# Feed-forwards by seven half-size block products for eight, in a two-block transformer kernel

## The reference

```python
hn = rms_norm(h, ln_mlp[layer])
h = h + jnp.square(jax.nn.relu(hn @ w_mlp1[layer])) @ w_mlp2[layer]
...
mod = c_act @ ada_w[layer] + ada_b[layer]
...
h = rms_norm_2(x, norm_mlp[layer]) * (1.0 + scale2) + shift2
x = x + gate2 * (jnp.square(jax.nn.relu(h @ mlp_w1[layer])) @ mlp_w2[layer])
```

## Time and profile before

| what | value |
|---|---|
| runs of the kernel | 2666.81, 2666.29, 2665.3 us; median 2666.29 |
| profiled execution | span 2664.3 us, 35686 instructions; some 2.0 us less than the median of the runs |
| TensorE matmul busy | 2627.4 us (99%), 12468 instructions |
| GpSimd busy | 1944.8 us (73%) |
| VectorE busy | 1268.0 us (48%) |
| ScalarE busy | 806.2 us (30%) |
| the four feed-forwards | from about 326 to 679, 1005 to 1358, 1676 to 2028 and 2309 to 2660 us of the span |

### The profile page before, as it was taken

How to read it: one execution, slowest core, us unless ns; L and a number is a source line. 1 busy time by engine, 2 the same in 40 slices (tenths; PEclk the granted TensorE clock), 3 DMA queues, 4 the chain that set the end, 5 groups by cost and what they waited for, 6 DMA issues and landing times.

```text
span 2664.3 us, 35686 instructions
## 1 busy us (share of the span) xinstructions
PE 2627.4 (99%) x12468; PEld 2069.3 (78%) x12468; DVE 1268.0 (48%) x1836; ACT 806.2 (30%) x1396; POOL 1944.8 (73%) x2832
## 2 busy tenths in 40 slices
PE   9999999999999999999999999999999999999999
PEld 6777788888766678888877888888887666788887
DVE  4766454442476655445234477511223776612211
ACT  4454311002255542101122254300113776401101
POOL 5533599998665559999876866887886555688875
PEclk9999999999999999999999999999999999999999
DMA  5211275653222126566322322333333211233332
GB/s 147 64 48 40 81 223 177 184 175 102 79 63 61 58 87 194 178 191 188 103 88 71 91 63 60 88 103 95 100 90 87 64 56 56 64 111 95 95 95 71
DMA packets 425151, 272.08 MB, mean 102 GB/s; under 512 B 9786, under 2 KB 411588, under 8 KB 425028
## 3 DMA queue, kind: packets, MB, share of 16 engines
q1 hardware_dynamic: 409154, 216.68, 28.1%
q10 hardware_dynamic: 15874, 53.67, 6.4%
HBM read 268.22 MB, written 2.10 MB: 101 GB/s over the span
## 4 chain that ended last, share of the span: by engine, by line
POOL 41%; PE 37%; issue 19%; DVE 1%; POOLq 1%; SPq 1%; DMA 0%; ACT 0%; DVEq 0%; ACTq 0%
POOL w_lo L400 28%; POOL w_hi L393 11%; PE ps L453 5%; PE ps L455 4%; PE ps L454 4%; PE pair L453 4%; PE pair L455 4%; PE pair L454 4%; POOL slot_mark L406 2%; PE ps L2041 2%; PE ps L2043 2%; PE ps L2042 2%; PE ps L1037 1%; PE pair L2451 1%; PE ps L1038 1%
## 5 line engine op out<-in xcount | busy, mean ns | idle before, releaser
L400 POOL TENSOR_TENSOR w_lo<-w_raw,w_hi 128x256 fp32r<-128x256 f32 x1612 | 1329.6, 856 | 33.6
L406 POOL TENSOR_TENSOR slot_mark<-slot_mark 128x1 f32<-128x1 f32 x400 | 98.9, 247 | 653.4 <-PE ps L455 346.8
L393 POOL TENSOR_SCALAR w_hi<-w_raw 128x512 fp32r<-128x512 f32 x806 | 533.6, 681 | 0.0
L453 PE MATMUL ps<-x_hi,w_hi 128*128 128x512 f32 x1040 | 423.5, 407 | 5.1 <-DVE x_lo L944 2.5
L455 PE MATMUL ps<-x_hi,w_lo 128*128 128x512 f32 x1040 | 406.1, 390 | 0.0
L454 PE MATMUL ps<-x_lo,w_hi 128*128 128x512 f32 x1040 | 405.3, 390 | 0.0
L1148 ACT ACTIVATE tt<-sq 128x512 f32<-128x512 f32 x128 | 81.1, 634 | 1029.5 <-DVE sq L1189 525.3
L453 PEld LDWEIGHTS ps<-x_hi,w_hi 128*128 128x128 f32 x1040 | 195.3, 188 | 52.6 <-issue 12.6
L454 PEld LDWEIGHTS ps<-x_lo,w_hi 128*128 128x128 f32 x1040 | 195.5, 188 | 42.5 <-issue 5.5
L455 PEld LDWEIGHTS ps<-x_hi,w_lo 128*128 128x128 f32 x1040 | 195.2, 188 | 42.0
L453 PE MATMUL pair<-x_hi,w_hi 128*128 128x512 f32 x544 | 212.2, 390 | 0.0
(11 more groups left out here) (442 smaller groups left out, 4396.0 us busy)
## 6 DMA issues: line engine op xcount, KB each, us to landing
w_raw<-in_w_mlp_dram SPq DMA_DIRECT2D x128, 512.0 KB, 4.1
w_raw<-in_mlp_w_dram SPq DMA_DIRECT2D x128, 512.0 KB, 4.0
arena<-in_ada_w_dram ACTq DMA_DIRECT2D x96, 512.0 KB, 4.0
w_raw<-in_w_in_ab_dram SPq DMA_DIRECT2D x28, 512.0 KB, 3.7
w_raw<-in_w_qkv_o_dram SPq DMA_DIRECT2D x24, 512.0 KB, 3.7
w_raw<-in_w_qkv_dram SPq DMA_DIRECT2D x24, 512.0 KB, 3.8
w_raw<-in_w_in_e_dram SPq DMA_DIRECT2D x23, 512.0 KB, 4.0
w_raw<-in_w_ple_gate_dram SPq DMA_DIRECT2D x16, 512.0 KB, 4.0
```

What stands on the lines that cost most here:

```text
L393: last = nc.gpsimd.tensor_scalar(w_hi[:, j, k, :], w_raw[:, j, k, :], 1.0, 1.0, ALU.mult, ALU.mult)
L400: last = nc.gpsimd.tensor_tensor(w_lo[:, j, k, :], w_raw[:, j, k, :], w_hi[:, j, k, :].bitcast(F32), ALU.subtract)
L406: nc.gpsimd.tensor_tensor(slot_mark[:, 0:1], slot_mark[:, 1:2], slot_mark[:, 1:2], ALU.subtract)
L453: nc.tensor.matmul(bank[:, :], w_hi[:, j, k, :], hi[:, k, :], start=(k == 0), stop=False)
```

## The change

The first product of a feed-forward is computed in part by a scheme of seven block products for eight (the variant of Strassen's with 15 sums). Of the 32 chunks of the inner width the first six ("std") stay as they were. The other 26 make 13 pairs (hp = 1 to 13). Over a pair the first product is a 2 by 2 block product: the two chunks by the even and the odd tiles of x, by the two halves of the tokens. P1 to P7 are seven products of a 512 by 128 block of weights or of a sum of blocks (S1 to S4) with a half of the tokens of x or of sums of x (T1 to T4); each is 12 narrow matmuls (four tiles by three passes). Of the second product, four pieces g0 to g3 of the pair before are laid between: TensorE's order in a pair is P1, P2, g0, P4, P5, P6, g1, P7, g2, P3, g3. The second product of a pair is over four tiles of the middle, g0 to g3 of pair hp giving four output tiles of h, each 12 wide matmuls. hp = 0, 14 and 15 have second products only. A feed-forward then has 912 wide and 1092 narrow matmuls.

The work around it in a pair:

- ScalarE makes all eleven high parts (lines 1468 and 1477, 128x512), copies P1, P6 and P7's running sums out of PSUM (line 1483, 128x256), squares the two output tiles and rounds them (1494, 1496; in the second block relu as well), and issues the modulation's loads.
- VectorE makes five of the seven low parts of the products (line 1636), the four sums of weights (1644 to 1655), the outputs' quarters (1661, 1667, 1673), in the first block the scaling with relu (1678), the low parts of the middle (1684) and the four adds into h (1690).
- GpSimd makes the low parts of P1, P2 and of g0 to g3, two 128x256 operations each, and no high parts after the std chunks.
- The modulation is spread over three feed-forwards instead of two: 32 products of 128x1024 in each (three, three and two to a pair in the first twelve pairs), in a ring of two slots instead of four.

At the start of a feed-forward VectorE makes the sums T of x (16 operations of 128x256, `t_sums`), ScalarE their high parts and VectorE their low parts (`t_low`, 128x1024), between the std chunks' outputs. The sums lie in `t_tiles`; `raw_extra`, a fifth slot for loads of weights, and the modulation's slots share that memory. The PLE loads move from the output projection to the feed-forward's end, and some loops are written out.

The core of the diff:

```diff
-        LAST_QUARTER = "last"
...
+        t_tiles = take([ND, T])
+        arena_at[0] = 16 * T
+        raw_extra = take([ND, P])
+        ada_w = take([2, D])
...
+        PAIR = ["P1", "P2", "g0", "P4", "P5", "P6", "g1", "P7", "g2", "P3", "g3"]
+        POOL_LOWS = ["P1", "P2", "g0", "g1", "g2", "g3"]
+        SUM_OF = {"P7": "S3", "P5": "S1", "P6": "S2", "P3": "S4"}
...
+            for hp in range(1, 14):
+                for which in range(2):
+                    n = 2 * (hp - 1) + which
+                    if n == 0:
+                        sp.wait_ge(*t_at(i, "lo3"))
+                    elif n < 3:
+                        sp.wait_ge(*std_cut(i, 3 + n))
...
+                    chunk(pair_load(hp, which)[0], 4 * (hp // 2 + 1) + 2 * (hp % 2) + which)
...
+            for hp in range(16):
+                for what in POOL_LOWS if 1 <= hp <= 13 else POOL_LOWS[2:]:
...
+                    for k in (slice(0, 2), slice(2, 4)):
+                        last = nc.gpsimd.tensor_tensor(half_slot(w_lo, n)[:, k, :], raw[:, k, :],
+                                                       half_slot(w_hi, n)[:, k, :].bitcast(F32), ALU.subtract)
...
+            def product(hp, what, out, b_hi, b_lo, start=True, stop=True):
+                n = place(hp, what)
+                pe.wait_ge(*(pool_cut(i, hp, what) if what in POOL_LOWS else low_cut(i, hp, what)))
+                hi, lo = half_slot(w_hi, n), half_slot(w_lo, n)
+                for t in range(4):
+                    nc.tensor.matmul(out, hi[:, t, :], b_hi[:, t, :], start=(start and t == 0), stop=False,
...
+            for c in range(4):
+                g_product(0, c)
+            for hp in range(1, 14):
...
+                product(hp, "P1", first_sum[:, FIRST], *x_block(0, FIRST))
...
+                product(hp, "P2", second_product[:, FIRST], *x_block(1, FIRST))
+                g_product(hp, 0)
...
+                product(hp, "P4", later_sums[:, FIRST], *t_block(T4))
+                product(hp, "P5", later_sums[:, SECOND], *t_block(T1))
+                pe.wait_ge(*snapped(i, hp, "P1"))
+                product(hp, "P6", first_sum[:, FIRST], *t_block(T2), start=False)
+                g_product(hp, 1)
+                pe.wait_ge(*snapped(i, hp, "P6"))
+                product(hp, "P7", first_sum[:, FIRST], *t_block(T3), start=False)
+                g_product(hp, 2)
+                pe.wait_ge(*pair_out(i, hp, "C2"))
+                product(hp, "P3", later_sums[:, SECOND], *x_block(1, SECOND), start=False)
+                g_product(hp, 3)
...
+            std_mid(3)
+            g_high(0, 2)
+            g_high(0, 3)
+            high(1, "P1")
+            high(1, "P2")
+            std_mid(4)
...
+            std_rest(3)
+            std_out(4)
+            std_rest(4)
+            std_out(5)
+            sums_13(1)
+            std_rest(5)
+            add(0, 0)
```

More of the change, by code:

```diff
@@ L427, in cut_stream, with cut_quads @@
                 cut_lo(pool, 0, j)
[L428 to L434, removed]
+            def cut_quads(first, end, mlps):
+                with pool.Fori(first, end) as q:
+                    for j in range(4):
+                        pool.wait_ge(*loaded(q, j, mlps))
+                        pool.wait_ge(*done(q - 1, j))
+                        slot_free()
+                        cut_hi(q, j)
+                        cut_lo(pool, q, j)
@@ L1154, in mlp_scalar @@
[L1154 to L1158 removed]
+                for k in range(ND):
+                    nc.scalar.activation(t_tiles[:, k, :], h[:, k, :], ACT.Identity, scale=norm_gain(norm_before, k)[0]
+                                         ).then_inc(t_act, 1)
+            std_mid(0)
+            t_high(0)
+            t_high(1)
@@ new lines, in mlp_scalar, with ada_ahead @@
+            g_high(1, 1)
+            for hp in range(1, 14):
+                ahead = hp + 1
+                products = ada_products(i, hp)
+                def ada_ahead(n):
+                    if n < len(products) and products[n] + 2 < 32 * (i + 1):
+                        ada_load_one(act, i, products[n] + 2)
+                high(hp, "P6")
+                snap(hp, "P1", snap_p1)
+                high(hp, "P7")
+                g_high(hp, 2)
+                ada_ahead(0)
+                high(hp, "P3")
+                g_high(hp, 3)
+                if hp < 13:
+                    high(ahead, "P1")
+                    high(ahead, "P2")
+                ada_ahead(1)
+                snap(hp, "P6", snap_q)
+                g_high(ahead, 0)
+                if hp < 13:
+                    high(ahead, "P4")
+                ada_ahead(2)
+                snap(hp, "P7", snap_v)
+                if hp < 13:
+                    high(ahead, "P5")
+                else:
+                    g_high(14, 1)
+                    g_high(14, 2)
+                pair_mid(hp, 1)
+                if hp < 13:
+                    g_high(ahead, 1)
+                else:
+                    g_high(14, 3)
+                pair_mid(hp, 0)
@@ new lines, in mlp_vector @@
+            mid_low(13, 0)
+            if i in (1, 2):
+                ada_finish(v, i - 1)
+            for hp in (14, 15):
+                for c in range(4):
+                    n = 4 * (hp - 14) + c
+                    if i == 3 and n == 7:
+                        finish_add(v, gate_col(layer2, 1, n))
+                    else:
+                        add(hp, c)
+                    if next_norm is not None:
+                        norm_add_behind(v, next_norm, n)
+            if i == 3:
+                finish_vector(v)
```

776 lines of the change are left out of this document (568 added, 208 removed).

## The result

The changed kernel takes 2677.07 us (median of four runs, 2676.23 to 2679.16) against 2666.41 before (four runs): ratio 1.0044, 95% interval 1.003 to 1.0057. The profiled execution has a span of 2674.4 us, 10.1 more than that of before. The range ended at 2668; the time lies outside it.

What follows compares the result with a forecast made beforehand. TensorE's matmuls were taken as the bound: 2664.3 us of span − 55 for narrow matmuls + 2 × 7.5 + 2 × 1 for start waits + 2 × 1.7 for the clock = 2629.7, with 2.0 around it about 2632 us; range 2596 to 2668.

Steps and rivals of the forecast that it cites:

- A floor which the loads set, and it lies under what 256 columns take: Narrow matmuls in pairs: loads set only a floor, so 256 columns take 116.9 ns, saving 13.8 us per feed-forward, 55 in all.
- The upper end, 148 ns: Narrow matmul's highest price, from a line through 128 columns (109 ns) and 512 columns (226.7 ns).
- The chain: Feed-forward start: T, load, ScalarE, VectorE's add delay the third second product; 10.7 us after T, waits 7.5 or 1 us.
- Sixteen 256-column sums (16 × 0.41): Feed-forward start: VectorE's sums T of x take 6.6 us of its 19.5 us list.
- rival B: Steady pairs: VectorE becomes the bound through contention with GpSimd, 60 us over the forecast, about 2692 us; chance 0.1.
- the sum for the first two: First two feed-forwards' start: list from 336.7 plus 19.5 + 10.7 − 1.3 ends at 365.6, a wait of 1 us each.
- TensorE gets there after two second products: Third feed-forward's start: TensorE reaches the third second product at 1717.9 and waits until 1725.4, 7.5 us; the fourth as much.
- The modulation's sum: Modulation's sum on TensorE: as many columns as before in twice the matmuls, costed at nothing.
- VectorE at nothing in the steady part: Steady pairs: VectorE's 17.0 to 20.6 us of work fits under TensorE's 20.7 us, so it costs nothing.
- the 1.7 us for the clock behind a long stop: Feed-forward starts: clock at 0.50 for 3.3 us after a stop loses half, 1.7 us at each of two long stops.
- C: Rival on narrow matmuls: the load is not hidden, 148 ns each, +20 us per feed-forward, 2767 us; chance 0.05.
- Rival A: Feed-forward start is hidden and the narrow matmul takes half a wide one's time, about 2600 us; chance 0.2.

Runs made afterwards that it cites:

- Run 1: The changed kernel with pair 1's first load sent to a weight slot that the sums T do not use; 2654.4 us, ratio 0.9960 to the kernel before.
- run 6: The changed kernel with block products over 192 of 256 columns and 64 of 128 weight columns, other outputs left out; 2582.9 us, one execution.
- run 2: The changed kernel with pair 1's first load in a slot T does not use, and VectorE's and ScalarE's start work reordered; 2640.8 us, ratio 0.9906.
- run 7: On top of run 2, the low parts of P1 and P2 made by VectorE instead of GpSimd; 2640.75 us, ratio 0.9907 to the kernel before.

## Why the prediction was wrong

*The narrow matmul.* "A floor which the loads set, and it lies under what 256 columns take", with 116.9 ns, was the first step that failed. It treats load and columns as two limits of which the larger counts. The row it came from had weights of two columns, and with real loads the distance is 120.0 ns, although the floor of 110 alone would allow 113 to 117. That is 1092 × 3.1 ns = 3.4 us per feed-forward, 13.5 in all, and the wide ones behind narrow ones add 52 × 0.13 = 6.8: 35 us saved in place of 55. The upper end, 148 ns, was far off; a line through the loaded 128 columns was no model either.

*The start of a feed-forward.* The chain was right: T, the load, ScalarE's squares, the add. Its place and its releaser are in the trace. That it ended where it was forecast, 1726.7 against 1725.4 in the third feed-forward, is luck: that feed-forward began 3 us sooner than before. Counted from the first wide matmul over x, TensorE could have begun the third second product after 39.1 us in the first two feed-forwards and 39.7 in the others; the first add ended after 44.6, 44.0, 51.7 and 51.6, where the forecast's own sums have 39.6 and 47.4. So this is the second step that failed, a mis-sized term: 34.8 us were lost up to the third second product where 17 stood, and 7 to the slow clock behind it where 3.4 stood, some 42 in place of 20.4.

- "Sixteen 256-column sums (16 × 0.41)" took a row from a quiet place. The sums have two inputs in SBUF, and most of them run beside GpSimd's cuts. GpSimd and VectorE in the third feed-forward:

```profile
1706.42 3.37 POOL L643 TENSOR_TENSOR w_lo<-w_raw,w_hi 128x256 fp32r<-128x256 f32 x4 [6.29 <-ACT w_hi L1468]
```

```profile
1706.46 1.86 DVE L1612 TENSOR_TENSOR arena<-arena 128x256 f32<-128x256 f32 x2
1708.25 1.83 DVE L1616 SCALAR_TENSOR_TENSOR arena<-arena,mod 128x256 f32<-128x256 f32 x2
1710.00 0.87 DVE L1621 SCALAR_TENSOR_TENSOR arena<-arena,mod 128x256 f32<-128x256 f32 x2
```

  Two of them take 1.8 us while GpSimd cuts and 0.87 behind it. The trace's summary of the first of these lines (ns min/median/max) has

```profile
L1612 DVE TENSOR_TENSOR arena<-arena x16: 439/957/979, 337.0 to 2343.2; 128x256 f32<-128x256 f32 x16
```

  The sixteen took 10.8, 10.6, 11.4 and 11.4 us where 6.6 stood; T's four low parts gave 1.1 to 2.1 of it back (4.6 to 5.6 us where 6.7 stood). I used that contention for 512 columns and for rival B, and left it out here. The Trainium skill ("GPSIMD Engine Reference", section "8. Key points") has GpSimd contend with VectorE instructions of two SBUF inputs; that rule bore on this step, and the trace agrees: 0.44 us at least, 0.96 where GpSimd is cutting.
- In the sum for the first two, the 1.3 us for ScalarE's square and copy of chunk 2 were forgotten; the trace has 1.36 us there. With the sums, T ends at 359.4 in the first instead of 354.9. The chain behind T takes 1.1 to 1.2 us more than the 10.7 forecast (the load 4.3 to 4.4 instead of 4.0): the add ends at 371.1 instead of 365.6, and the wait is 5.5 us where I had 1.
- The clock fell behind all four stops, and was added for two.

"TensorE gets there after two second products", 1717.9, is wrong as well, but cost nothing of its own: in the third and fourth it had waited twice before, 2.91 us and 1.30 us in the third. T's sums had pushed the output of chunk 3, which frees the first bank, and its low part behind themselves on VectorE. I followed VectorE's list for the last thing in it, and not for what stood in the middle. These waits, and the clock that fell behind them, lie ahead of an add which does not depend on them; without them TensorE would have waited as much longer for the add. Run 1 bears this out for the clock: it falls there in the third feed-forward and not in the fourth, and both starts cost 8.2 us (run 1's windows):

```profile
1696.00:1716.00 20.00, 15.22 (x53) 11.27 (x52) 16.13 (x22) 10.59 (x17) 12.52 (x14) 0.83 0.42 131
2327.00:2347.00 20.00, 12.61 (x55) 9.57 (x55) 15.90 (x23) 10.59 (x17) 12.05 (x13) 1.00 0.26 79
```

*The modulation's sum* stood at nothing, with "as many columns as before in twice the matmuls"; it cost 2 us.

*Right:* all pairs but one run without a wait and alike with and without modulation, but for its sums, so VectorE at nothing in the steady part held; so did the 1.7 us for the clock behind a long stop (1.6). The sign is that of rivals B and C, but not by their causes: B's needs a shorter pair than 21.09 us to count (run 6), C's a narrow matmul above 129.5 ns. It is the forecast's own mechanism with both terms short, by 20 us and 21 us, which together are 41 of the 45 us that the forecast was out and more than the 34 it had. Rival A's hidden start is run 2 in two of four feed-forwards. Run 2 closes the account: its matmuls save 35 us where 55 stood, its starts cost some 8 us where 20.4 stood, and the modulation's sums 2 where nothing stood, 2632 + 20 − 12 + 2 = 2642; 2640.8 was measured.

## What to carry to other kernels

- Price a smaller matmul from one that has its own full weight load. Where load and columns took nearly the same time, the distance was above both (120.0 ns, against a floor near 110 and 114 with half the load); half as many columns cost 53% (120.0 of 226.7 ns), and seven for eight leaves 3% of a pair, not 5%.
- A scheme that saves a few per cent in the steady part has that little to pay its start with. Four starts gave back all of it here; a slot for the first load that nothing else uses and a list in the order in which the waiting engine needs things were worth 36 us.
- When a list grows on an engine, walk through it for every release in it, with the durations of the stretch in which it will run.

## What the runs showed of the hardware that I had not expected

- A matmul of 192 columns took 110 to 112 ns with weights of 128 columns, about as much as one of 128 columns (109), and 89 ns with weights of 64.
- In run 2, while VectorE ran two-input operations back to back, two GpSimd pieces took 4.96 us together; one that no VectorE operation overlaps takes 0.735 us in the median:

```profile
1701.68 4.96 POOL L644 TENSOR_TENSOR w_lo<-w_raw,w_hi 128x256 fp32r<-128x256 f32 x2 [5.29 <-ACT w_hi L1478]
```

- Two low parts of each pair can move between GpSimd and VectorE without any change of the time (run 7): VectorE took 24 operations more in 5.7 us, since its other operations got shorter when GpSimd did less.
